# The order of GpSimd's adding transfers in the down projection of a two-layer decoder trunk

## What is computed

```python
def conv_ffn(x, norm_g, w_up, conv_w, conv_b, w_down):
    h = rms_norm(x, norm_g)
    a, b = jnp.split(h @ w_up, 2, axis=-1)
    a = lax.conv_general_dilated(...) + conv_b
    return (jax.nn.silu(a) * b) @ w_down
```

## Time and profile before

| | us |
|---|---|
| median of 3 runs | 1582.34 (1582.21 to 1583.85) |
| the profiled execution | 1581.26 |
| its span, first to last instruction | 1579.5 |
| PE busy in it | 1566.5 (99%) |
| DVE busy | 1171.5 (74%) |
| ACT busy | 769.3 (49%) |
| GpSimd busy | 250.6 (16%) |

### The profile page before, as it was taken

One profiled execution on the slowest core, in us unless ns is written; L12 is line 12 of the kernel. 1 busy time (PEld: TensorE's weight loads), 2 busy tenths in 40 slices (PEclk: granted clock), 3 DMA queues, 4 the chain that ended last, 5 costly groups with the idle time before them and its releaser, 6 DMA issues. The chain is left out here.

```text
span 1579.5 us, 22764 instructions
## 1 busy us (share of the span) xinstructions
PE 1566.5 (99%) x9106; PEld 1383.8 (88%) x9106; DVE 1171.5 (74%) x1295; ACT 769.3 (49%) x982; POOL 250.6 (16%) x270
## 2 busy tenths in 40 slices
PE   9999999999999999999999999999999999999998
PEld 7888888888888999999988888888888899999776
DVE  7257876786679877796972678658756898777877
ACT  5344334542355555664533533355332565556646
POOL 4000000000230222241240000000002212223310
PEclk9999999999999999999999999999999999999999
DMA  5332222222227888899223322222222388888991
GB/s 195 99 122 75 79 81 93 80 68 93 94 94 240 239 233 237 264 239 260 97 96 104 114 75 78 81 94 70 78 94 93 100 251 237 237 237 277 229 271 64
DMA packets 66628, 231.41 MB, mean 147 GB/s; under 512 B 7392, under 2 KB 7904, under 8 KB 66528
## 3 DMA queue, kind: packets, MB, share of 16 engines
q1 hardware_dynamic: 52272, 182.93, 33.4%
q0 software_dynamic: 12096, 41.95, 14.7%
q10 hardware_dynamic: 2160, 5.12, 1.1%
HBM read 225.78 MB, written 2.10 MB: 144 GB/s over the span
## 5 line engine op out<-in xcount | busy, mean ns | idle before, releaser
L1748 PE MATMUL ps<-u_hi,w_hi 128*128 128x512 f32 x768 | 301.3, 392 | 0.0
L1749 PE MATMUL ps<-u_lo,w_hi 128*128 128x512 f32 x768 | 299.3, 390 | 0.0
L1750 PE MATMUL ps<-u_hi,w_lo 128*128 128x512 f32 x768 | 299.1, 390 | 0.0
L1186 DVE TENSOR_TENSOR w_lo<-w_raw,w_hi 128x1024 fp32r<-128x1024 f32 x158 | 208.6, 1333 | 68.3 <-ACT w_hi L752 67.9
L752 ACT ACTIVATE w_hi<-w_raw 128x1024 fp32r<-128x1024 f32 x158 | 164.3, 1052 | 76.6 <-DMA w_raw<-wts 70.2
L1754 PE MATMUL ps<-comb_hi,far_hi 128*128 128x256 f32 x688 | 194.5, 283 | 0.0
L1755 PE MATMUL ps<-comb_lo,far_hi 128*128 128x256 f32 x688 | 194.1, 282 | 0.0
L1756 PE MATMUL ps<-comb_hi,far_lo 128*128 128x256 f32 x624 | 175.7, 282 | 0.0
L1750 PEld LDWEIGHTS ps<-u_hi,w_lo 128*128 128x128 f32 x768 | 144.2, 188 | 30.4
L1748 PEld LDWEIGHTS ps<-u_hi,w_hi 128*128 128x128 f32 x768 | 144.4, 188 | 28.4
L1749 PEld LDWEIGHTS ps<-u_lo,w_hi 128*128 128x128 f32 x768 | 144.4, 188 | 28.3
(11 more groups left out here) (325 smaller groups left out, 3402.6 us busy)
## 6 DMA issues: line engine op xcount, KB each, us to landing
w_raw<-wts SPq DMA_DIRECT2D x212, 512.0 KB, 3.5
far_raw<-wts SPq DMA_DIRECT2D x56, 512.0 KB, 3.6
t_raw<-wdn POOLq DMA_DIRECT2D x30, 512.0 KB, 9.8
w_raw<-wdn SPq DMA_DIRECT2D x24, 512.0 KB, 7.0
w_raw<-wts POOLq DMA_DIRECT2D x18, 512.0 KB, 10.3
far_raw<-wts POOLq DMA_DIRECT2D x16, 512.0 KB, 7.0
far_raw<-wdn SPq DMA_DIRECT2D x16, 512.0 KB, 8.3
t_raw<-wdn SPq DMA_DIRECT2D x10, 512.0 KB, 5.9
```

The source lines that it names most:

```text
L1186: nc.vector.tensor_tensor(w_lo[:, s, :], w_raw[:, s, :], w_hi[:, s, :].bitcast(F32), ALU.subtract).then_inc(s_lo, 1)
L1748: nc.tensor.matmul(dst, a_hi, b_hi, start=start, stop=False)
L1749: nc.tensor.matmul(dst, a_hi, b_lo, start=False, stop=False)
L1750: return nc.tensor.matmul(dst, a_lo, b_hi, start=False, stop=stop)
```

## The change

In `further_sums` the six adding transfers for the slots of units 24 to 29 now come directly after those of W22 to `t_raw`, and the six of W21 are woven between and behind them: A24, A25, A26, W21-0, A27, W21-1, A28, W21-2, A29, W21-3, W21-4, W21-5. The counts of `s_tsum[j]` follow: A(24+j) now waits for 32 and brings it to 48, W21-j waits for 48, that is until A(24+j) has landed, and brings it to 64. ACT's waits in `unit_high` are turned round to match (fifth product 48, seventh 64). Nothing is added or removed: the same transfers move the same bytes.

```diff
@@ further_sums(l) @@
-                for k, quarter in ((1, W22), (2, W21)):
-                    for j in range(PIECES):
-                        pool.wait_ge(s_qlo, l * UNITS_DOWN + k * PIECES + j + 1)
-                        add_piece(l, j, quarter)
                 for j in range(PIECES):
-                    u = 4 * PIECES + j
-                    s = RAW_SLOT[l][u]
-                    pool.wait_ge(s_tsum[j], l * 64 + 48)
-                    pool.wait_ge(s_fetch[s], 16 * (1 + l * arrivals_of_layer(u) + arrivals(u)))
-                    nc.gpsimd.dma_start(unit_raw(l, u), wdn[l * 4 + W22, :, j * 1024:j * 1024 + piece(j)],
-                                        accum_op=ALU.add).then_inc(s_tsum[j], 16)
+                    pool.wait_ge(s_qlo, l * UNITS_DOWN + PIECES + j + 1)
+                    add_piece(l, j, W22)
+                for j in range(PIECES + 2):
+                    if j < PIECES:
+                        u = 4 * PIECES + j
+                        s = RAW_SLOT[l][u]
+                        pool.wait_ge(s_tsum[j], l * 64 + 32)
+                        pool.wait_ge(s_fetch[s], 16 * (1 + l * arrivals_of_layer(u) + arrivals(u)))
+                        nc.gpsimd.dma_start(unit_raw(l, u), wdn[l * 4 + W22, :, j * 1024:j * 1024 + piece(j)],
+                                            accum_op=ALU.add).then_inc(s_tsum[j], 16)
+                    if j >= 2:
+                        pool.wait_ge(s_qlo, l * UNITS_DOWN + 2 * PIECES + j - 2 + 1)
+                        pool.wait_ge(s_tsum[j - 2], l * 64 + 48)
+                        add_piece(l, j - 2, W21)
@@ unit_high(l, u) @@
-                    act.wait_ge(s_tsum[j], l * 64 + {1: 16, 2: 32, 6: 48}[k])
+                    act.wait_ge(s_tsum[j], l * 64 + {1: 16, 2: 32, 6: 64}[k])
                 elif k == 4:
-                    act.wait_ge(s_tsum[j], l * 64 + 64)
+                    act.wait_ge(s_tsum[j], l * 64 + 48)
```

## The result

The changed kernel takes 1597.59 us (median of 4 runs, 1596.62 to 1599.82). The kernel before takes 1582.98 us beside it (1582.21 to 1583.85). The ratio is 1.0096, with a 95% interval of 1.0084 to 1.0109. The sign was forecast, the size was not. The loss is 14.6 us where 7.0 were expected, and the time lies above the range.

A forecast was written before the change was run, and what follows sets the result against it. The prediction took PE's work plus its waits (2.5 us winnable) to bound the kernel. Added waits at units 28 and 29, (3.0 + 1.4) + (1.2 + 1.4) = 7.0 us, on 1582.3 gave 1589.3 us, range 1583 to 1595.

The forecast's parts named there:

- What bounds the kernel: Whole kernel: PE's work plus its waits; 2.5 us of down-projection waits are winnable, through chain L26, A26, A27, A28, unit 28.
- L26 takes 3.7 us: Load ahead of A26: 3.7 us instead of 6.2 with the six W21 additions gone, so A26 lands earlier.
- Four steps of 13.8 us from A26 to A28: GpSimd's queue: W21-0, A27, W21-1, A28 land in turn, 3.0 + 3 x 3.6 us; A28 +3.0 us (layer 1), +1.2 (layer 0).
- The sentence on L27 and L28: Between A26 and A28: both loads land before their turn comes, so no transfer is held by its own wait.
- A29 6.1 us behind A28: GpSimd's queue: W21-2 ahead of A29 adds one 3.6 us step, plus a half step for the half piece.
- A second wait of 1.4 us at unit 29: PE, each layer: unit 29 is ready 1.4 us after PE has done unit 28.
- W21-3 to W21-5 cost nothing: Behind A29: they land by about 1551 in an empty stretch, free unless late by more than ten us.
- The slower string: Rival: steps between landings take 4.0 to 4.4 us because loads share the stretch; 1593 to 1598 us, chance 0.08.
- Cancel: Rival: 3.0 us for all four steps, so earlier start and added transfers offset each other; 1583 us, chance 0.15.
- fit in: Rival: steps stay at 2.5 us, A28 is no later, PE's waits vanish; about 1580 us, chance 0.08.
- The falling clock: Rival: PE's clock drops from 2.4 to 1.2 GHz during longer waits; 1591 to 1593 us, chance 0.15.
- My 1.8 us for a slow stretch: PE after a clock drop: one slow stretch like the eight warm-up matmuls costs 1.8 us.

The follow-up runs named there:

- two_early: The changed kernel with W21-0 and W21-1 directly behind A25, then A26 to A29 together, then W21-2 to W21-5; 1579.44 us, ratio 0.9993.
- fill3: The changed kernel with three groups of useless PE matmuls: six ahead of unit 28's wait, two each ahead of units 29 and 30; 1596.32 us, ratio 1.0088.
- one group of fillers: The changed kernel with six useless PE matmuls ahead of unit 28's wait in each layer; 1597.76 us, ratio 1.0097.
- behind_a27: The changed kernel reordered from A26 on to A26, A27, W21-0, A28, W21-1, A29, then W21-2 and on; 1591.07 us, ratio 1.0052.
- one_between: The changed kernel with W21-1 moved behind A28, so the order is A26, W21-0, A27, A28, W21-1, A29; 1592.35 us, ratio 1.0073.
- w21_last: The changed kernel with all six W21 transfers moved behind A29, none between A26 and A29; 1580.43 us, ratio 0.9996.

## Why the prediction was half right

Two steps failed. The price of the steps was too low: 13.8 us from A26 to A28, where the trace has 16.1 and 15.2. And the path behind A29 was followed to unit 29 alone, with 1.4 us there, where it goes on to unit 30. That unit came 7.6 and 8.5 us late, where the forecast had 2.6 and 4.4 in all. The parts in order:

**What bounds the kernel**: right. The loss lies in PE's waits in the two down projections, and in the slow matmuls behind them. The chain L26, A26, A27, A28, unit 28 is the right one, and PE started unit 28 3.35 and 3.3 us behind A28's landing, as read before.

**L26 takes 3.7 us**: right, 3.6 and 3.5 (731.3 - 727.73, 1527.9 - 1524.42). A26 landed 6.5 and 6.7 us behind its issue, against 6.0. On the scale of before, that is less 1.27 us in layer 0 and 9.97 in layer 1 (the shift of L28's issue), it landed at 737.0 and 1525.1, against 736.7 and 1524.7.

**Four steps of 13.8 us from A26 to A28**: too short. They took 754.4 - 738.3 = 16.1 and 1550.3 - 1535.1 = 15.2 us. So A28 came 3.8 and 4.8 us later than before, against 1.2 and 3.0. I had taken 3.0 to 3.6 us for a step from a kernel in which nothing but A27 stood between A26 and A28. The measured mean is 4.0 and 3.8, inside the bounds that I had named (2.5 to 4.4), near the dear end. The first step, for which I took 3.0 because few loads are out, was 4.0 and 4.4. The loads share the string more than I thought. In layer 0 of the change W21-1, A28, W21-2 and A29 landed at 750.5, 754.4, 758.2 and 760.8, and L30, L31, L32 and L33 each 0.2 us behind one of them (750.7, 754.6, 758.3, 761.0). So a step of 3.8 us carried an addition and a load, where an addition alone takes 2.5. The sentence on L27 and L28 was half wrong: L28 landed at 744.3 and 1540.0 and GpSimd waited for it. The filled kernel shows that the wait is not what made A28 late, since with less than half of it (3.85 us instead of 8.45) A28 landed at the same distance. Why L28 became slow is partly shown: holding A26 back made it fast again (3.6 and 4.6 us), and with W21-0 behind A26 it was mostly slower (9.7 to 10.8 where `two_early` had 5.9 and 8.1). But `fill3`, with the order of the change, had 6.3 and 7.9, so the order alone doesn't settle it.

**A29 6.1 us behind A28**: right, 6.4 and 6.3.

**A second wait of 1.4 us at unit 29**: here the mechanism failed. The wait itself was sized well: at full clock, with one group of fillers, unit 29 waits 1.46 and 1.48 us. But I followed A29 to unit 29 and stopped there. Behind it ACT and DVE, which work in order, have unit 30 still to make. DVE's rows in the changed kernel, from the low part of unit 29 on:

```profile
1557.32 0.69 DVE L1408 TENSOR_TENSOR far_lo<-far_raw,far_hi 128x512 fp32r<-128x512 f32 x1 [3.88 <-ACT far_hi L867]
1557.93 1.22 DVE L1437 TENSOR_TENSOR s_raw<-s_raw,g_raw 128x1024 f32<-128x1024 f32 x1
1559.06 1.22 DVE L1408 TENSOR_TENSOR w_lo<-w_raw,far_hi 128x1024 fp32r<-128x1024 f32 x1
1560.27 1.23 DVE L1419 TENSOR_TENSOR comb_lo<-s_raw,comb_hi 128x1024 fp32r<-128x1024 f32 x1
```

They are the low part of unit 29, the sum of two chunks, unit 30's low part and the chunk's low part, which releases unit 30. From A29's landing to unit 30 that is 765.85 - 760.8 = 1561.64 - 1556.6 = 5.0 us. Wherever PE waits at unit 30 in the experiments, the distance is the same 5.0. Before, the landing of A29 in layer 0, issued at 738.98, and the starts of unit 30 were:

```profile
far_raw<-wdn POOLq DMA_DIRECT2D x1, 256.0 KB, 13.0
...
757.01 0.36 PE L1754 MATMUL ps<-comb_hi,far_hi 128*128 128x256 f32 x1
...
1543.13 0.41 PE L1754 MATMUL ps<-far_hi,comb_hi 128*128 128x512 f32 x1
```

The distance was 757.01 - 752.0 = 5.0 us in layer 0 and 1543.13 - 1538.0 = 5.1 in layer 1. So the path had at most 0.1 us of slack then, though no wait showed, and every us that A29 is late is a us of time.

**The sum again, with these two steps mended.** Unit 30 is late by A29's delay. My own landings of A29 (1544.6 and 756.6) with 5.0 us behind them give 1549.6 and 761.6 instead of 1543.1 and 757.0, 6.5 + 4.6 = 11.1 us in place of 7.0. A29 really landed another 2.0 us later in layer 1 and 2.9 in layer 0 (at 1546.6 and 759.5 on the scale of before), of which the four steps are 1.4 and 2.3 and the rest is A26 and the last step. That gives 16.0. The trace has unit 30 at 1561.64 - 9.97 = 1551.67 and 765.85 - 1.27 = 764.58, so 8.5 + 7.6 = 16.1 us. That is the profiled execution, the slowest of four. The medians differ by 14.6. The two profiled spans differ by 18.5; the other 2.4 us are drifts ahead of the two stretches, the slow clock at the head of layer 1's projection among them. So of the error in this execution about 4.1 us are the missing path and 4.9 us the prices ahead of A29.

**W21-3 to W21-5 cost nothing**: right, no wait of PE lies behind unit 30 in the stage.

**The rivals.** The slower string (1593 to 1598, 0.08) holds the time, but that is partly luck: its steps were to be 4.0 to 4.4 us and were 3.8 and 4.0, and it too left out the path to unit 30. "Cancel" and "fit in" fell with the price of a step, since none of the eight between A26 and A28 took less than 3.2 us. The falling clock (0.15) came true as an event and not as a cost. Between 1554.57 and 1555.00 two matmuls with 512 columns start 0.43 us apart, near the 0.45 of the warm-up:

```profile
1554.57 0.63 PE L1760 MATMUL ps<-far_hi,chunk_lo 128*128 128x512 f32 x1
1555.00 0.63 PE L1758 MATMUL ps<-far_hi,chunk_hi 128*128 128x512 f32 x1
```

PE worked unit 28 slowly and unit 29 had come meanwhile, hence no wait there. Unit 30 was bound to A29 anyway, and the kernel with three groups of fillers shows that full clock in these waits is worth 1.3 us at the most. My 1.8 us for a slow stretch was near what one costs where nothing hides it (1.6 us, with one group of fillers). The Trainium skill, "TensorE: Matmul & The Clock Gate", section "Part 1: The HAM clock gate", lets the array drop to 1.2 GHz after idling. By that rule the event was to be expected, and the trace agrees with 0.50 behind a wait of 5.5 us.

**What a transfer of W21 ahead costs.** By the table, A29 is 18.0 and 18.3 us behind L28's issue with none ahead, 22.8 to 25.8 with two, 27.3 and 26.7 with three. That is (27.3 - 18.0) / 3 = 3.1 and (26.7 - 18.3) / 3 = 2.8 us each with three. With two it is 2.4 and 2.8 in `behind_a27`, 3.5 and 3.7 in `one_between`. An addition alone takes 2.5 us, and the 3.8 us of a step in the change are more than 3.1 or 2.8 because they contain a load that lands ahead of A29 in `w21_last` as well (L28 to L32 in both). The formula of the Trainium skill, "DMA: Bandwidth & Descriptors", section "Anatomy of one DMA — SWDGE (gpsimd) path", comes to an estimated 1.2 us of moving for 512 KB. The traces disagree, with 2.4 us at the least for each further addition.

**What stays open.** Two kernels with the same numbers ahead (1, 2) differ by 2.2 us at A28 and about 2 at A29, so the place of W21-0 against A27 counts too. The landings go with that: in `one_between` six loads (L28 to L33) had landed ahead of A29 in both layers, in `behind_a27` four and five. No run holds the loads fixed, so this is read from the traces and not tested. Nor is it shown what sets the order in which loads and additions land, and so why L28 takes from 3.6 to 10.8 us.

## What to carry to other kernels

In a queue that lands its transfers in order, a transfer that nobody needs soon costs about its own length (2.4 to 3.7 us here) to each one behind it that somebody waits for. Put the urgent ones first and let the others follow, whatever idle room that leaves further ahead. When a late arrival is followed to its consumer, go on to the next consumers of the same in-order engines, and compare each with before: a path without a wait may have no slack. An order that makes a transfer wait for the landing of its neighbour (W21-0 behind A24) can leave too little in the queue, and the work then falls into the next crowd.

## What the runs showed of the hardware

An adding transfer of 512 KB takes 2.5 us of the queue alone, and 3.8 with a load beside it. One more ahead of A29 delays it by 2.4 to 3.7 us. A plain load of the same size takes 3.4 to 3.7 us when no addition runs. Beside additions L28 took 5.9 and 8.1 us in `two_early` and 10.8 and 10.1 in the change, and the loads that SP issues behind it, faster than they land, took more: 11.5 for L30 and 15.5 for L34 in layer 0 of the change. Where loads and additions ran together, as in the rows on the clock above, the transfer engines moved 262 to 298 GB/s at a share above 1.0, against 211 for additions alone.

In the waits of 5.5 us at unit 28 of the change the granted clock of PE fell from 2.4 to 1.2 GHz. In layer 1 PE stopped at 1548.1, the mean over 1550 to 1552 was 0.68, and 0.50 over 1552 to 1556. Some 4 us after PE had started again it was back. In the kernel with one group of fillers it fell at unit 30 instead (0.50 over 766 to 768 and over 1560 to 1562), behind waits of only 0.9 to 2 us that came one after the other, and cost 1.6 us of the trace in layer 1. At the head of layer 1's projection it fell with a wait of 2.5 us in the change and stayed at 1.00 with one of 2.9 before, so the length of one wait alone doesn't tell whether it falls.
